# Encoder layer with experts: the first expert's tokens chosen by comparing ranks, and a new order for the work of the first expert

## The reference

```python
def expert_choice_ffn(h, w_router, w_exp_gate, w_exp_up, w_exp_down):
    aff = jax.nn.softmax((tok @ w_router).astype(jnp.float32), axis=-1)
    cap = EC_CAPACITY_FACTOR * N // N_EXPERTS            # 2 * 512 // 16 = 64 tokens
    gate, idx = lax.top_k(aff.T, cap)                    # each of 16 experts takes its 64 best
    xs = tok[idx]
    hid = silu(einsum('ecd,edf->ecf', xs, w_exp_gate)) * einsum('ecd,edf->ecf', xs, w_exp_up)
    out = einsum('ecf,efd->ecd', hid, w_exp_down) * gate[..., None]
    y = jnp.zeros((N, D)).at[idx.reshape(-1)].add(out.reshape(-1, D))
```

## Time and profile before

| quantity | value |
|---|---|
| time, three runs | 2385.63, 2387.12, 2387.31 us |
| median | 2387.12 us |
| time of the profiled execution | 2386.68 us |
| span of its trace | 2384.8 us |
| TensorE busy | 2360.4 us (99%) |
| VectorE busy | 1624.6 us (68%) |
| ScalarE busy | 1488.6 us (62%) |
| from the first expert's start on, TensorE | busy all the time |

### The profile page before, as it was taken

One profiled execution on the slowest core, in us unless ns is written; L12 is line 12 of the kernel. 1 busy time (PEld: TensorE's weight loads), 2 busy tenths in 40 slices (PEclk: granted clock), 3 DMA queues, 4 the chain that ended last, 5 costly groups with the idle time before them and its releaser, 6 DMA issues.

```text
span 2384.8 us, 33778 instructions
## 1 busy us (share of the span) xinstructions
PE 2360.4 (99%) x11804; PEld 1967.3 (82%) x11804; DVE 1624.6 (68%) x1767; ACT 1488.6 (62%) x1707; POOL 401.4 (17%) x279
## 2 busy tenths in 40 slices
PE   8999999999999999999998999999999999999998
PEld 7888888888888888888885888888888888888886
DVE  5545464634546455455346988888888888888897
ACT  5656564533466465554335777777777777777776
POOL 1533433000053324320002000000000000000000
PEclk9999999999999999999999999999999999999999
DMA  6413321125432224112238999999999999999998
GB/s 189 128 45 100 88 73 67 70 98 204 158 98 83 83 62 126 64 63 80 90 155 334 403 393 382 383 383 381 390 387 393 387 383 383 385 387 376 394 375 326
DMA packets 214395, 557.35 MB, mean 234 GB/s; under 512 B 11968, under 2 KB 93376, under 8 KB 209216
## 3 DMA queue, kind: packets, MB, share of 16 engines
q1 hardware_dynamic: 207280, 530.89, 60.4%
q0 software_dynamic: 7056, 25.69, 3.6%
HBM read 533.47 MB, written 23.07 MB: 233 GB/s over the span
## 4 chain that ended last, share of the span: by engine, by line
PE 97%; DVE 1%; DMA 0%; issue 0%; ACT 0%; POOLq 0%; SPq 0%; DVEq 0%; ACTq 0%
PE bank L1433 44%; PE bank L1073 15%; PE bank L1118 13%; PE bank L1039 7%; PE bank L1062 5%; PE bank L1093 3%; PE bank L1236 2%; PE bank L1479 2%; PE bank L1134 2%; PE bank L1217 1%; PE bank L1156 1%; PE bank L1197 1%; PE bank L1203 1%; PE bank L1160 1%; PE bank L1252 0%
## 5 line engine op out<-in xcount | busy, mean ns | idle before, releaser
L2575 DVE TENSOR_TENSOR m_lo<-m_raw,m_hi 128x2048 fp32r<-128x2048 f32 x380 | 867.4, 2290 | 121.0 <-ACT m_hi L1925 117.4
L1925 ACT ACTIVATE m_hi<-m_raw 128x2048 fp32r<-128x2048 f32 x382 | 733.6, 1921 | 261.5 <-PE bank L1433 256.6
L1433 PE MATMUL bank<-m_hi,xs_hi 128*128 128x512 f32 x1032 | 321.0, 392 | 0.0
L1433 PE MATMUL bank<-m_hi,xs_lo 128*128 128x512 f32 x1032 | 317.9, 389 | 0.0
L1433 PE MATMUL bank<-m_lo,xs_hi 128*128 128x512 f32 x1032 | 317.8, 389 | 0.0
L2063 DVE TENSOR_TENSOR w_lo<-w_raw,w_hi 128x1152 fp32r<-128x1152 f32 (+4 forms) x110 | 145.0, 1344 | 180.1 <-ACT w_hi L1561 180.0
L1433 PEld LDWEIGHTS bank<-m_lo,xs_hi 128*128 128x128 f32 x1032 | 193.7, 188 | 40.5
L1433 PEld LDWEIGHTS bank<-m_hi,xs_lo 128*128 128x128 f32 x1032 | 193.7, 188 | 40.4
L1433 PEld LDWEIGHTS bank<-m_hi,xs_hi 128*128 128x128 f32 x1032 | 191.4, 188 | 38.2 <-DVE xs_lo L2597 0.2
L1073 PE MATMUL bank<-h_hi,w_hi 128*128 128x512 f32 x512 | 203.0, 396 | 0.0
L1073 PE MATMUL bank<-h_lo,w_hi 128*128 128x512 f32 x512 | 199.6, 390 | 0.0
(11 more groups left out here) (292 smaller groups left out, 4239.4 us busy)
## 6 DMA issues: line engine op xcount, KB each, us to landing
m_raw<-in_w_exp_gate SPq DMA_DIRECT2D x128, 1024.0 KB, 8.1
m_raw<-in_w_exp_up SPq DMA_DIRECT2D x128, 1024.0 KB, 7.6
m_raw<-in_w_exp_down SPq DMA_DIRECT2D x128, 1024.0 KB, 7.4
w_raw<-in_w_b SPq DMA_DIRECT2D x66, 512.0 KB, 6.2
w_raw<-in_w_a SPq DMA_DIRECT2D x24, 1024.0 KB, 5.1
w_raw<-in_w_c SPq DMA_DIRECT2D x24, 1024.0 KB, 4.8
w_raw<-in_w_d SPq DMA_DIRECT2D x8, 1024.0 KB, 6.5
xt<-in_x SPq DMA_DIRECT2D x8, 512.0 KB, 7.9
```

Source lines behind the costliest of these rows:

```text
L1433: mm = pe.matmul(ps[:, half, :], a[:, chunk + k, :], v[:, k, 512 * half:512 * (half + 1)], start=first and k == n == 0, stop=last and k == ...
L1925: act.activation(m_hi[slot.slot][:, :, :], m_raw[raw.slot][:, :, :], ACT.Copy)\
L2575: dve.tensor_tensor(m_lo[slot.slot][:, :, :], m_raw[raw.slot][:, :, :], m_hi[slot.slot][:, :, :].bitcast(F32), ALU.subtract)\
```

## The change

The change chooses the first expert's tokens in another way, and moves the eight rounds, which now serve the other fifteen experts, into the first expert's work.

- **First expert's tokens.** The affinities to expert 0 are multiplied by 2 to the 64th (`raised`), and TensorE spreads them to all partitions by four transposes per request (`t`). For each tile of 128 tokens VectorE compares all tokens' values with the tile's own in one instruction that subtracts, compares with a margin that decides ties, and sums (`r`, `compared`: 512, 384, 256 and 128 columns; half of the pairs are not compared but counted by TensorE in `c`). Each token's rank gives a 0/1 mark per slot (`o`, `hot`), and small matmuls with these marks give index and weight of each slot (`q`), which `p` writes to `index_get`. For the first request all this stands between the D tiles, for the second behind the softmax. A table (`rank_table`, 784 columns) is loaded for it.
- **Weights.** SyncE issues units 0 and 1, and unit 2 only when the gather has landed; before it was the eighth unit that waited for it.
- **GpSimd** does the subtraction of units 0 and 8, after the gather is issued.
- **VectorE** does rounds 0 to 3, then the remainder of `xs`, unit 1, rounds 4 and 5, units 2 to 6, rounds 6 and 7 with the merge, unit 7, and on.
- **TensorE** turns the lists behind unit 9. The first expert is written out apart from the loop: units 0 to 3, 4 to 7, 8 to 11, transposes of `hid`, 12 to 15, down 16 to 19, transposes of the next `xs`, transposes of `hid`, down 20 to 23, and only then the second expert. ScalarE and VectorE have the same order. `keep_busy` between the rounds is gone.

The diff, cut to its core:

```diff
-WARM_START, WARM_FIRST, WARM_GATHER, WARM_SPLIT, WARM_NORM = 3, 1, 6, 2, 4
-WARM_ROUNDS = {1: 1, 2: 1, 3: 1, 4: 1, 5: 1, 6: 1, 7: 1}
+WARM_START, WARM_FIRST, WARM_GATHER, WARM_SPLIT, WARM_NORM = 3, 1, 4, 2, 4
...
-EARLY_SPLITS = 2
+POOLED = (0, 8)
+RAISE = 2.0 ** 64
...
+        if last and i == NT - 2:
+            out += [("h", 0), *(("t", 0, i) for i in range(NT))]
+    if last:
+        out += [("r", 0, j) for j in range(NT)]
...
-                ("E", 2), ("E", 3), ("e", 2), ("b", 0), ("e", 3), ("B", 3)]
+                ("t", 1, 1), ("E", 2), ("E", 3), ("e", 2), ("t", 1, 2), ("e", 3), ("t", 1, 3), ("q", 0), ("b", 0),
+                ("Z", 1), ("r", 1, 0), ("r", 1, 1), ("r", 1, 2), ("r", 1, 3), ("c", 1), ("o", 1), ("q", 1), ("p", 1),
+                ("B", 3)]
...
+                    sp.dma_start(rank_table[:, :], rope_r_c[:, 2 * T + P:]).then_inc(s_rank_table, 16)
...
-                if unit.k == RAW_SLOTS - 1:
+                if unit.k == 2:
 
                     sp.wait_ge(s_gather, 16)
+                    sp.wait_ge(s_picked, 2 * NB)
...
-            for i in range(EARLY_SPLITS):
-                pool.wait_ge(s_mhi, i + 1)
-                pool.tensor_tensor(m_lo[i][:, :, :], m_raw[i][:, :, :], m_hi[i][:, :, :].bitcast(F32),
-                                   ALU.subtract).then_inc(s_mlo, 1)
...
+            for n, k in enumerate(POOLED):
+                raw, cut = k % RAW_SLOTS, k % SPLIT_SLOTS
+                pool.wait_ge(s_mhi, k + 1)
+                pool.wait_ge(s_rounds, n + 1)
+                pool.tensor_tensor(m_lo[cut][:, :, :], m_raw[raw][:, :, :], m_hi[cut][:, :, :].bitcast(F32),
+                                   ALU.subtract).then_inc(s_plo, 1)
+
+            pool.wait_ge(s_route, 2)
...
+                elif what == "t":
+
+                    of = arg[0]
+                    if i == 0:
+                        all_read(pe, s_out_free, outs)
+                        all_read(pe, s_proj_free, proj, but=0 if of else 2)
+                    pe.wait_ge(s_raised, of * (1 + i) + 1)
+                    pe.transpose(ranked[of][:, natural(i)], raised[:, of, i:i + 1].to_broadcast([P, P]), ident[:, :])\
+                        .then_inc(s_rows, 1)
+                elif what == "c":
+
+                    if i == 0:
+                        all_read(pe, s_sc_free, sc)
+                    for j in range(NT - 1, 0, -1):
+                        pe.wait_ge(s_beats, i * NT + NT - j)
+                        for k in range(j):
+                            last = pe.matmul(counts[i], beats[j][:, natural(k)], unit_cols[:, k, :],
+                                             start=j == NT - 1 and k == 0, stop=j == 1)
+                    last.then_inc(s_counts, 1)
+                elif what == "q":
+
+                    pe.wait_ge(s_hot, 2 * i + 1)
+                    mine = slice(CAP * i, CAP * (i + 1))
+                    for k in range(NT):
+                        for part in range(2):
+                            last = pe.matmul(pick[mine, :], hot_16[:, i, k, :], tokens_16[:, i, k, part:part + 1],
+                                             start=k + part == 0, stop=k + part == NT)
+                    last.then_inc(s_picked, 1)
...
-            for k, times in enumerate(WARM_ROUNDS.values()):
-                pe.wait_ge(s_round, k + 1)
-                keep_busy(times, ps_proj[:, 0, :])
-            for a in (chosen_at, chosen):
-                pe.wait_ge(s_best, 1)
-                pe.wait_ge(s_tr_free[tr.slot], START + tr.lap)
-                pe.transpose(ps_tr[0:CAP, tr.slot, 0:48], a[0:48, :], ident[0:48, 0:48]).then_inc(s_tr, 1)
-                tr.k += 1
             keep_busy(WARM_GATHER, ps_proj[:, 0, :])
...
-            with rolled(pe, NE - 1, mt, {"unit": 24, "slot": 24, "tr": 6, "step": 2}) as e:
-                expert(e, False)
+            gate_cols(lists=True)
+            hidden_transposes(1)
+            up_cols()
+            down(0, 0, hid_hi, hid_lo)
+            token_transposes(32)
+            hidden_transposes(2)
+            down(0, 1, hid_hi, hid_lo)
+            operand_ready()
+            gate_cols()
+            up_cols()
+            with rolled(pe, NE - 2, mt, {"unit": 24, "slot": 24, "tr": 6, "step": 2}) as e:
+                expert(e, False, shift=1)
...
+            def compared(of, nth):
+
+                j, cols = NT - 1 - nth, P * (NT - nth)
...
+                if nth == 0:
+                    dve.wait_ge(s_rows, NT * (of + 1))
+
+                dve.scalar_tensor_tensor(beats[j][:, :], ranked[of][:, 0:cols], raised[:, of, j:j + 1], margins[:, T - cols:],
+                                         ALU.subtract, ALU.is_gt, accum_out=row_sum[:, of, j:j + 1]).then_inc(s_beats, 1)
...
+                elif what == "h":
+                    dve.tensor_scalar(raised[:, i, :], aff[:, :, 0], RAISE, None, ALU.mult).then_inc(s_raised, 1)
...
+                elif what == "p":
+                    dve.wait_ge(s_picked, 2 * NB - 1)
+                    dve.tensor_copy(index_get[:, 0:1], pick).then_inc(s_first, 1)
+                    dve.tensor_copy(m_index[:, 0:1], pick)
...
-            dve.wait_ge(s_asked, 1)
-            dve.wait_ge(s_mlo, EARLY_SPLITS)
...
+            dve.sem_inc(s_rounds, 1)
+            eight_best(0)
+            eight_best(1)
+            eight_best(2)
+            eight_best(3)
+            split_unless_pooled()
+            transposed_lo(xs_hi, xs_lo)
             split_units(1)
+            eight_best(4)
+            eight_best(5)
+            split_units(2)
+            after()
+            split_units(3)
+            dve.sem_inc(s_rounds, 1)
+            eight_best(6)
+            eight_best(7)
+            halves_merged()
+            split_units(1)
+            after()
+            split_unless_pooled()
+            split_units(2)
+            hidden_step()
```

More of the change, by code:

```diff
@@ L602, in tile_read, with lo_ready @@
             eng.wait_ge(s_proj_free[proj.slot], START + proj.lap + 1)
+        def lo_ready(eng, unit, behind=0):
+            k = unit.k - behind
+            if k in POOLED:
+                eng.wait_ge(s_plo, POOLED.index(k) + 1)
+            else:
+                eng.wait_ge(s_mlo, unit.n(1 - behind - sum(each < k for each in POOLED)))
         def all_stored(eng, count):
@@ L1310, in seam_step @@
                     pe.matmul(logits[i], parts[i % 2], fold[:, :], start=True, stop=True).then_inc(s_logit, 1)
+                elif what == "t":
[23 more added lines that the diff above has]
+                    last.then_inc(s_picked, 1)
+                    pe.wait_ge(s_hot, 2 * i + 2)
+                    for k in range(NT):
+                        last = pe.matmul(pick_gate[mine, :], hot[:, i, k, :], raised[:, i, k:k + 1],
+                                         start=k == 0, stop=k == NT - 1)
+                    last.then_inc(s_picked, 1)
                 elif what == "b":
@@ L1965, in expert @@
                 split_units()
[L1967 to L1973 removed]
+                output_scaled(e)
             def result_square(i):
@@ L2038, in _ @@
             split_units()
+            after()
+            split_units()
+            swish_step()
+            transposed_hi(hid_hi)
+            after()
+            split_units()
+            after()
+            split_units()
+            transposed_hi(xs_hi)
+            transposed_hi(hid_hi)
+            after()
+            split_units()
+            output_scaled(0)
+            after()
+            split_units()
+            swish_step()
+            after()
+            split_units()
             per = {"raw": 24, "slot": 24, "unit": 24, "done": 24, "tr": 6, "step": 2}
-            with rolled(act, NE - 1, mt, per) as e:
-                expert(e)
+            with rolled(act, NE - 2, mt, per) as e:
+                expert(e + 1)
             last_expert()
@@ L2532, in _, with eight_best @@
             all_read(dve, s_tr_free, tr)
-            for r in range(CAP // 8):
+            def eight_best(r):
                 eight = slice(8 * r, 8 * r + 8)
@@ L2691, in _ @@
             split_units()
+            after()
+            split_units(2)
             hidden_step()
+            split_units(2)
             per = {"raw": 24, "slot": 24, "unit": 24, "done": 24, "tr": 6, "step": 2}
-            with rolled(dve, NE - 1, mt, per):
+            with rolled(dve, NE - 2, mt, per):
                 expert()
@@ L2724, in rope_tables, with ranks @@
         out.append(np.stack([np.cos(angle), sign * np.sin(angle)], axis=1).astype(f))
-    out[0] = np.concatenate([out[0].reshape(P, 2 * T), swaps().T.astype(f)], axis=1)
+    out[0] = np.concatenate([out[0].reshape(P, 2 * T), swaps().T.astype(f), ranks().astype(f)], axis=1)
     return out
+def ranks():
+    p = np.arange(P)
+    slot = np.broadcast_to((np.arange(CAP)[None, :] - P * np.arange(NT - 1, -1, -1)[:, None]).reshape(1, -1), (P, NT * CAP))
+    before = p[None, :] <= p[:, None]
```

(6 more changed lines are left out.)

176 lines of the change are left out of this document (126 added, 50 removed), and 1 row of the table out.

## The result

| | time, us | span, us |
|---|---|---|
| before, median of four | 2387.22 (2385.63 to 2387.47) | 2384.8 |
| changed, median of four | 2410.89 (2409.59 to 2411.30) | 2409.1 |

The changed kernel takes 1.0099 times as long, 95% interval 1.0083 to 1.0115. The forecast was 2408.8 us, slower by 0.9%.

What follows compares the result with a forecast made beforehand. TensorE was taken to bound the kernel (97% of the chain), so its waits are paid in full. Terms 1.2 + 3.6 + 4.3 + 2.6 + 1.0 + 6.4 + 2.6 = 21.7 us gave 2408.8 us, range 2398 to 2414.

Steps and rivals of the forecast that it cites:

- first product, against before: Start of the first expert on TensorE: 1.2 us later than before, the hold outweighing the gather's lead of 8.0 us.
- VectorE up to unit 7: First expert: remainders, rounds and merge on VectorE make unit 7 ready at 23.1 us instead of 19.5, cost 3.6 us.
- standstill beside GpSimd: At the merge, VectorE stands still until GpSimd's subtraction of unit 8 is done; unit 7 comes 4.3 us later.
- clock behind it: After the long TensorE idle stretches before units 7 and 20, the clock falls to half speed: 2.6 us each.
- unit 20: First expert's second half: VectorE's remainders and the shared PSUM tile for transposes of `hid` delay unit 20 by 6.4 us.
- The closing: End of the second request: a TensorE wait, added transposes and counting matmuls cost 2.2 us, bounds 1.5 and 3.
- The chain: From last softmax tile to gathered rows: index at 1268.3, rows used at 1274.3 instead of 1284.53, before the closing's cost.
- The hold: ScalarE converts late-loaded units 2 and 3 before writing `xs_hi`, so the rows wait: 9.2 us, bounds 8 and 12.
- No standstill: Rival at units 7 and 8: VectorE and GpSimd don't block each other, clock stays; 14.8 us, 2401.9; chance 0.2.
- the clock stays up: Rival: TensorE's clock does not fall in idle stretches of 5 us; 16.5 us, 2403.6; chance 0.12.
- The hold is short: Rival before the first product: transfers of units 2 and 3 land with the rows; 15.0 us, 2402; chance 0.06.
- The early gather pays: Rival: the lead of 8.0 us is kept up to the second expert, 2379.1 us; chance 0.04.

Runs made afterwards that it cites:

- three parts undone: Changed kernel with the gather waited for at unit 7, unit 8 back on VectorE, and the old order of the first expert's second half: 2387.85 us.
- the last two kernels: Three parts undone, rounds spread, gather waited for at unit 3: 2382.54 us; the same without the multiplication before the counts: 2381.84 us.

## Why the prediction was right, and where not

| step | predicted | measured |
|---|---|---|
| first product, against before | +1.2 | +2.5 |
| VectorE up to unit 7 | 3.6 | 2.9 |
| standstill beside GpSimd | 4.3, at unit 7 | 6.1, at unit 8 |
| clock behind it | 2.6 | 3.1 |
| unit 14 | 1.0 | 1.0 |
| unit 20 | 6.4 | 6.6 |
| clock behind it | 2.6 | 2.0 |
| sum | 21.7 | 24.2 |

The measured column is made from starts in TensorE's timeline of the changed kernel; it is one execution, and the changed kernel's median is 2.1 us above the forecast. Unit 7 begins 22.37 us after the first product (19.48 in the old order); from unit 7 to unit 8 there are 8.86 instead of 2.72; from unit 8 to the transposes 14.02 for four units of 2.72 (this holds the lists' turning too, so that 3.1 is the clock and some tenths); to the `xs` transposes 23.63 for 0.89 and eight units; from there to unit 20 8.42 for 1.78; and 45.48 to the next `hid` transposes for sixteen units.

**The closing** costs 2.0 us, predicted 2.2: the seventh D tile is added at 1257.11 where it was 1256.02, and the third, ahead of the new work, stood 0.88 us earlier in this trace. The wait behind the third tile is 1.0. The whole trace was 0.9 us early there, which lies in earlier stages and hides some of the chain's loss.

**The chain** was sized well: compares 2.0 us, index at 1270.55 (2.0 of closing, less that 0.9, added to the 1268.3 of the prediction gives 1269.4), gather issued 1.14 later, used 5.29 after that. The missing 1.1 us is the one multiplication between the last transposes and the counts, 1.92 us at half clock: VectorE waits 1.98 us for the counts. I had not counted it. Nor had I counted the wait for the store of `normed`. It lands at 1270.2 (issued at 1261.23, 9.0 us), just ahead of the index, and the gather can't be issued before it. Without the multiplication the gather would have come some 0.4 us sooner and not 1.1; in seven of the eleven runs the store lands last, if only just in some. How the choice is made sets the gather's time only as long as it ends behind that store.

**The hold** is the right step with a size too small: 10.1 us instead of 9.2. Unit 2 was converted at 1283.46, 6.6 us after its issue; I took the 4.8 us of the earlier trace rows. Six transfers were issued within 4.8 us, and in the windows from 1278 to 1282 the queues moved 240 and 287 GB/s, against 424 later; how much of the delay is sharing and how much a slow start was not tried apart. The distance to the next conversion, 2.57 us, is the one of the earlier trace rows.

**VectorE up to unit 7** cost 2.9 of 3.6 us, but TensorE shows a wait of only 0.19 us there. The clock, which had fallen in the hold, explains it, in the windows of TensorE from the first product on:

```profile
1288.00:1290.00 2.00, 0.72 (x2) 0.50 1.02 408
1290.00:1292.00 2.00, 2.00 (x6) 0.50 1.03 410
1292.00:1294.00 2.00, 2.00 (x6) 0.50 1.02 410
1294.00:1296.00 2.00, 2.00 (x7) 0.66 1.03 412
1296.00:1298.00 2.00, 2.00 (x11) 1.00 1.02 406
```

TensorE ran its first units at 1.2 GHz: units 0 and 1 took 8.42 us instead of 5.88. This lies beside VectorE's lateness, as the prediction had it for the first unit. With three parts undone, where TensorE started at full clock, VectorE's lateness comes out as waits of 1.77 and 0.64 us at units 2 and 7, and unit 7 begins 22.33 us after the first product, as here (22.37). But the clock has a price of its own: in the run in which VectorE fills the hold it is not late, and unit 7 still begins after 20.94 us instead of 19.48.

**The standstill** is the step whose mechanism was half wrong. I had VectorE waiting for GpSimd, at the merge, and unit 7 late. In the profiled execution VectorE was 0.22 us ahead, GpSimd stood still and unit 8 was late. VectorE was through the merge 20.1 us after the first product, where the prediction's terms give 20.8 (a round takes 1.38 us, not 1.48), and GpSimd began at 20.3 instead of 19.5; either error alone would have left the order as predicted. In the runs with the old order and with eight multiplications it came as predicted: VectorE stood still at the merge, and unit 7 began 26.7 us after the first product, forecast 27.4. The Trainium skill ("SBUF — State Buffer", section "Who interferes with whom") has the later of the two blocked. The traces agree both ways: VectorE's 4.55 us where GpSimd was first, GpSimd's 10.83 where VectorE was first. What I had not drawn from it is that a row of VectorE's subtractions counts as one: in these traces GpSimd got in only at a pause or at `hid` with its operand in PSUM. The sum suffered a little: with its clock the standstill of GpSimd cost 6.1 + 3.1 us against 4.3 + 2.6 forecast, and this, with the hold, is most of what the sum lacks.

**Unit 20 and the clock** hold as predicted. The test with four multiplications puts 2.1 us on the clock there; the test with eight shows that they must fit in the wait. The clock's price there is not fixed: from unit 20 to the next `hid` transposes the excess over sixteen units is 1.6 to 2.9 us in the five traces with this wait left as it was, and 0.1 and 0.2 in the two with it filled.

**The rivals.** "No standstill" is settled by the run without GpSimd's unit 8 (6.1 us), "the clock stays up" by the four multiplications. "The hold is short" is refuted by the trace. "The early gather pays" was refuted for this change, and holds for the last two kernels: everything behind the landing then costs less than the lead, which is 7.9 and 8.6 us there.

**Slips in the working.** The sum without the standstill is 14.8 us, as under the rivals, and not 14.9. The 2399 us of a short hold without a standstill doesn't follow from the terms, which give 2395 with the clock up behind it and 2398 without. Neither enters the forecast.

**What stays open.** How much of the 4.7 us between the kernels with the wait at unit 7 and at unit 3 belongs to the gather, and how much to the lists, which were turned one unit earlier in the same step, was not tried apart; the traces have 3.9 us less from gather issue to rows, and 1.6 us less of waiting for the second gather. That the gather lands 4.3 to 5.2 us after its issue with nearly empty queues and 8.3 beside unit loads goes with full queues in the traces; whether it waits behind the loads or shares with them they don't show. No run moved the store of `normed`, so what an earlier index would be worth without it is not known.

## What to carry to other kernels

A result that is ready sooner is worth nothing if an engine's written order puts waited-for work in front of its first consumer: look at what stands between the landing and the use on each engine in turn. Between "load everything" and "load nothing" ahead of a latency-critical small transfer there is a middle, and with it came the only kernels here that beat the one before (the lists were turned a unit earlier in the same step). When a step is made faster, look at what else its consumer waits for: here the store of the very rows to be gathered. And an idle engine is no free help: GpSimd's subtraction beside VectorE's cost 6.1 us net to save 2.24 of VectorE's.

## What the runs showed of the hardware

- A GpSimd subtraction of 128x2048 (4.53 us beside VectorE's rounds) took 10.83 us beside three VectorE subtractions that followed each other at once, and 10.86 in a second kernel with the same order up to there; where VectorE paused, 5.65 and 5.82. Each was done 4.43 to 4.46 us after the end of VectorE's subtractions.
- VectorE's addition of 64x64 elements, 0.22 us where GpSimd was idle, took 4.52 to 4.55 us when GpSimd had begun its subtraction 0.1 us before.
- A gather of 128 rows of 4 KB landed 4.3 to 5.2 us after its issue with nearly empty queues and 8.2 to 8.4 us after it while unit loads kept them at 400 GB/s and more. The 512 KB store of the last tile of `normed`, issued while the first unit loads were under way, landed 7.9 to 10.6 us after its issue.
- Multiplications that keep TensorE's clock at 2.4 GHz through a wait of 4.2 us gave back 2.1 us (2.4 in the traces); filling past the end of the wait took them away again.
